# MLA stage of a two-layer block: transposes of two probability blocks together in every even unit

## The reference

```python
def attend(blk):
    qn, qr = blk
    s = (jnp.einsum('bqhd,bkhd->bhqk', qn, k_nope, preferred_element_type=jnp.float32)
         + jnp.einsum('bqhr,bkr->bhqk', qr, k_rope, preferred_element_type=jnp.float32)) * scale
    p = jax.nn.softmax(s, axis=-1).astype(v.dtype)
    return jnp.einsum('bhqk,bkhd->bqhd', p, v)
o = lax.map(attend, (to_blocks(q_nope), to_blocks(q_rope)))
```

## Time and profile before

| | us |
|---|---|
| median of 3 runs | 3247.91 (3247.35 to 3248.86) |
| the profiled execution | 3250.53 |
| its span, first to last instruction | 3248.9 |
| TensorE busy | 3220.4 |
| VectorE, ScalarE, GpSimd busy | 1803.5, 1305.8, 630.8 |

### The profile page before, as it was taken

One profiled execution on the slowest core, in us unless ns is written; L12 is line 12 of the kernel. 1 busy time (PEld: TensorE's weight loads), 2 busy tenths in 40 slices (PEclk: granted clock), 3 DMA queues, 4 the chain that ended last, 5 costly groups with the idle time before them and its releaser, 6 DMA issues.

```text
span 3248.9 us, 38219 instructions
## 1 busy us (share of the span) xinstructions
PE 3220.4 (99%) x15436; PEld 2691.3 (83%) x15436; DVE 1803.5 (56%) x2728; ACT 1305.8 (40%) x1991; POOL 630.8 (19%) x502
## 2 busy tenths in 40 slices
PE   9999999999999999999999999999999999999998
PEld 7888888888888888888888888888888888788887
DVE  6865775444448655845443465554544268974433
ACT  5653553332237534633322323332332248743221
POOL 1521231111005311520110022111111014521101
PEclk9999999999999999999999999999999999999999
DMA  4122323323221122322233222222223223223222
GB/s 137 38 81 65 109 93 104 100 99 100 96 93 59 60 75 90 109 94 95 96 99 107 91 81 81 82 91 91 97 92 100 95 81 102 91 89 101 97 98 85
DMA packets 85136, 295.60 MB, mean 91 GB/s; under 512 B 9568, under 2 KB 12128, under 8 KB 84960
## 3 DMA queue, kind: packets, MB, share of 16 engines
q1 hardware_dynamic: 84384, 292.76, 27.4%
q10 hardware_dynamic: 576, 0.40, 0.0%
HBM read 291.02 MB, written 2.10 MB: 90 GB/s over the span
## 4 chain that ended last, share of the span: by engine, by line
PE 85%; DVE 8%; ACT 3%; issue 1%; POOL 1%; DMA 1%; SPq 0%; ACTq 0%; DVEq 0%; POOLq 0%
PE bank L313 84%; DVE wl L569 2%; PE bank L316 2%; DMA raw<-in_wts 1%; DVE small L1299 1%; ACT m_p L536 1%; POOL u_g L591 1%; ACT wh L533 1%; DVE u_uc L565 0%; DVE m_ptl L569 0%; DVE c_kl L569 0%; DVE m_qf L559 0%; DVE m_sh L809 0%; DVE u_h L3283 0%; ACT m_pth L533 0%
## 5 line engine op out<-in xcount | busy, mean ns | idle before, releaser
L569 DVE TENSOR_TENSOR wl<-raw,wh 128x1024 fp32r<-128x1024 f32 (+1 forms) x531 | 660.1, 1246 | 761.7 <-ACT wh L533 760.8
L313 PE MATMUL bank<-zh,wh 128*128 128x512 f32 (+1 forms) x2652 | 1025.9, 387 | 6.2 <-ACT zh L533 6.2
L313 PE MATMUL bank<-zh,wl 128*128 128x512 f32 (+1 forms) x2652 | 1020.7, 385 | 1.9 <-DVE wl L569 1.9
L313 PE MATMUL bank<-zl,wh 128*128 128x512 f32 (+1 forms) x2652 | 1019.1, 384 | 1.7 <-DVE zl L572 1.6
L533 ACT ACTIVATE wh<-raw 128x1024 fp32r<-128x1024 f32 (+1 forms) x531 | 555.9, 1052 | 531.4 <-PE bank L313 469.0
L313 PEld LDWEIGHTS bank<-zh,wl 128*128 128x128 f32 x2652 | 499.6, 188 | 107.2 <-DVE wl L569 7.2
L313 PEld LDWEIGHTS bank<-zh,wh 128*128 128x128 f32 x2652 | 500.0, 189 | 102.5 <-ACT zh L533 6.2
L313 PEld LDWEIGHTS bank<-zl,wh 128*128 128x128 f32 x2652 | 500.0, 189 | 98.2 <-DVE zl L572 3.0
L313 PE MATMUL bank<-f_mh,wh 128*128 128x512 f32 (+1 forms) x748 | 285.1, 381 | 0.0
L313 PE MATMUL bank<-f_mh,wl 128*128 128x512 f32 (+1 forms) x748 | 283.3, 379 | 0.0
L313 PE MATMUL bank<-f_ml,wh 128*128 128x512 f32 (+1 forms) x748 | 280.7, 375 | 0.0
(11 more groups left out here) (337 smaller groups left out, 4474.3 us busy)
## 6 DMA issues: line engine op xcount, KB each, us to landing
raw<-in_wts SPq DMA_DIRECT2D x529, 512.0 KB, 3.3
c_nb<-in_c_bias SPq DMA_DIRECT2D x16, 384.0 KB, 3.2
x<-in_xT SPq DMA_DIRECT2D x8, 256.0 KB, 6.2
out<-x SPq DMA_DIRECT2D x13, 128.0 KB, 1.8
b_mask<-in_b_mask SPq DMA_DIRECT2D x2, 576.0 KB, 4.5
r_d<-in_decay SPq DMA_DIRECT2D x4, 256.0 KB, 2.9
raw<-in_wts SPq DMA_DIRECT2D x2, 256.0 KB, 3.7
m_t<-in_mla_tab SPq DMA_DIRECT2D x2, 256.0 KB, 4.7
```

The source lines that it names most:

```text
L313: return self.e.matmul(out, l, r, start=start, stop=stop, skip_group_check=inside)
L569: return self.e.tensor_tensor(out, src, b32(hi), ALU.subtract)
```

## The change

- TensorE: from unit 4 on, each even unit i transposes blocks i - 4 and i - 3, one group of four after the other, ahead of its scores; odd units transpose nothing. Unit 33 goes, and block 30 is transposed in unit 34 beside 31.
- The tuple of tiles from `fill` is (0, 2, 0, 1, 1, 2, 0, 2), where it was (0, 1, 1, 1, 2, 1, 1, 1): odd units take more, even ones fewer; eight in eight units, as before.
- ScalarE copies block i - 4 in iteration i, not block i - 3.
- VectorE makes the low half of block i - 4 in iteration i: in odd iterations ahead of the reduction, in even ones behind it, where the low half was always.

```diff
--- before.py
+++ after.py
@@ -1207,8 +1207,7 @@
     rest, q = fill(), queries()
 
     def unit(i):
-        if 3 <= i < 35:
-            j = i - 3
+        for j in (i - 4, i - 3) if 4 <= i < 35 and i % 2 == 0 else ():
             ps = L.claim(turn_bank(j), "lo", "pt", "mla", l, j)
             L.wait_ge("sc", "mla", l, j)
             for kt in range(4):
@@ -1241,12 +1240,12 @@
             next(q, None)
         if i % 8 == 3 and i < 24:
             tensor_k(L, l, i // 8 + 1)
-        for _ in range((0, 1, 1, 1, 2, 1, 1, 1)[i % 8]):
+        for _ in range((0, 2, 0, 1, 1, 2, 0, 2)[i % 8]):
             next(rest, None)
 
     for i in range(32):
         unit(i)
-    return {0: lambda: unit(32), 1: lambda: unit(33), 2: lambda: unit(34), 4: lambda: unit(36)}
+    return {0: lambda: unit(32), 2: lambda: unit(34), 4: lambda: unit(36)}
 
 
 def turn_bank(j):
@@ -1261,8 +1260,8 @@
             scalar_b(L, ("b", l, 0) + MLA_FILL[i // 8 - 1])
         if i >= 9 and i % 4 == 1:
             scalar_y_move(L, m.m_yt, (i - 9) // 4, "mla", l)
-        if 3 <= i < 35:
-            j = i - 3
+        if 4 <= i < 36:
+            j = i - 4
             hb = j // 2
             L.wait_ge("tp", "mla", l, j)
             if hb > 1:
@@ -1286,6 +1285,16 @@
     L.ahead()
 
 
+def vector_pt_lo(L, l, i):
+
+    m, j = L.m, i - 4
+    if 0 <= j < 32:
+        hb = j // 2
+        hi, lo = [f4(x)[:, :, 128 * (j % 2):128 * (j % 2) + 128] for x in m.m_pt[hb % 2]]
+        L.wait_ge("hi", "pt", "mla", l, j)
+        L.lo(lo, f4(m.bank[turn_bank(j)]), hi).then_inc(*L.tell("lo", "pt", "mla", l, j))
+
+
 def vector_mla(L, l):
     m = L.m
     L.lead = 0
@@ -1293,6 +1302,8 @@
         level = L.level
         if i == 29:
             vector_y_add(L, m.m_yt, m.m_yf, 5, "mla", l)
+        if i % 2:
+            vector_pt_lo(L, l, i)
         if i < 32:
             c = i % 8
             L.wait_ge("qk", "mla", l, i)
@@ -1301,12 +1312,8 @@
             vector_mv(L, l, (0, 3, 1, 2)[i])
         if i >= 9 and i % 4 == 1 and i != 29:
             vector_y_add(L, m.m_yt, m.m_yf, (i - 9) // 4, "mla", l)
-        if 3 <= i < 35:
-            j = i - 3
-            hb = j // 2
-            hi, lo = [f4(x)[:, :, 128 * (j % 2):128 * (j % 2) + 128] for x in m.m_pt[hb % 2]]
-            L.wait_ge("hi", "pt", "mla", l, j)
-            L.lo(lo, f4(m.bank[turn_bank(j)]), hi).then_inc(*L.tell("lo", "pt", "mla", l, j))
+        if i % 2 == 0:
+            vector_pt_lo(L, l, i)
         if i < 32:
             vector_div(L, i, "mla", l)
         L.ahead_of(level)
```

## The result

The changed kernel takes 3278.42 us (median of 4 runs, 3277.48 to 3279.72), the kernel before beside it 3247.75 us. The ratio is 1.0095, 95% interval 1.0083 to 1.0106: 30.7 us more. The forecast was 3271.4, a loss of 23.5 us: direction and range held, and 7.2 us of the loss were missing.

A forecast was written before the change was run, and what follows sets the result against it. TensorE, 99% busy, bounds the kernel, but in MLA VectorE's lengthened loop would set the pace: 11.8 us per layer, 23.6 for two, less 0.1 for switches, on 3247.9 gives 3271.4 us; range 3257 to 3281 (80%).

The forecast's parts named there:

- The bound: MLA: VectorE's serial loop through ScalarE would set the pace, walked unit by unit at 26.4 us per eight units against 22.4.
- Eight transposes together: TensorE in MLA: grouping removes 32 switches between transposes and products; saving taken as 0, upper bound 2.6 us.
- the sum for switches: Closing total: 0.1 us subtracted for switches from 23.6 us, giving +23.5 us.
- Weight tiles dealt anew: TensorE's tiles in MLA: new dealing evens out units, costs nothing itself; still eight tiles per eight units.
- Low half ahead of the reduction: VectorE, odd MLA iterations: low half leaves the exp's cover and waits for its copy; 4.0 us more per eight units.
- keeps its place before the exp: ScalarE in MLA: remark that the copy m_pth, now a unit on, stays ahead of the exp; no cost given.
- The order of SP's loads is the same, so TensorE's own work does not change: SP's load queue: unchanged order was taken to leave TensorE's work as it was, at no cost.
- the banded stage that follows, which I take as unchanged: Stage after MLA: assumed to take the same time; a time change there was named as a sign of error.
- The clock: Rival for both MLA stages: TensorE's clock falls to its lower level for half of them, 3355 us; chance 2%.
- The signs in the profile: MLA: five expected traces, among them m_ptl waits nearly every even unit, 10 to 13 us per layer, and TensorE busy 85.
- Faster: Rival in MLA: vanished m_pth waits pay for uncovered low halves, stalls go, switches save up to 2.6; 3240 us, chance 6%.
- No change: Rival in MLA: VectorE's loop lengthens by less than its lead, TensorE stays the bound; 3247.9 within 6 us, chance 8%.

The follow-up runs named there:

- experiment 7: Changed kernel, but both copies and both low halves of a pair made in the even iteration, behind the reduction, none in odd ones: 3254.89 us, ratio to before 1.0020.
- experiments 4 and 9: Changed kernel with the old dealing of tiles: 3277.77 us; kernel before with the new dealing alone: 3247.82 us.
- experiment 2: Kernel before, with VectorE's low half (block i - 3) ahead of the reduction in odd iterations: 3271.06 us, ratio to before 1.0072.
- experiment 6: Kernel before, with copies and low halves of block i - 4 instead of i - 3 in iteration i, behind the reduction: 3272.50 us, ratio to before 1.0075.
- experiment 3: Changed kernel, with SP's b_mask load waiting for the transposes of block 30, not the low half of block 31: 3272.89 us.
- experiment 1: Changed kernel, with the low half of odd blocks behind the reduction again, as for even blocks: 3268.25 us, ratio to before 1.0063.

## Why the prediction was right, and where it was short

- *The bound.* Right: VectorE, 56% busy on the page, sets the pace of MLA through its round trip to ScalarE. Its walk gave 26.4 us for eight units, and 26.5 was traced; reductions 16, 24 and 31 were walked at 112.9, 139.3 and 160.6 and came at 113.22, 139.73 and 161.13; the late start after the stage was 11.9 for 11.4.
- *Eight transposes together.* Right: nothing saved (experiment 7). The walk took 0 for a switch and yet took 0.1 off the sum for switches; that term has no source, and it changes nothing. The Trainium skill ("TensorE: Matmul & The Clock Gate", Part 2) has only an isolated product pay for its drain, while in a stream it is hidden. The rows of experiment 7 agree: 0.67 and 1.11 us leave no break at a change between transposes and products.
- *Weight tiles dealt anew.* Right: nothing, in either kernel (experiments 4 and 9).
- *Low half ahead of the reduction.* The mechanism holds (experiment 2, 23 us by itself). But "Here the price sits" said too much: undoing it returned only 10 us. The part on the dealing passed over the copies' move with "keeps its place before the exp", and that move, which takes a unit of lead from the low half, costs 24 us alone (experiment 6, where it falls on every block; in the changed kernel it falls on odd ones). The two causes don't add: the late mask load apart, which is about 5 us of the changed kernel, either of them makes up most of the loss, and with the low halves early and half of them covered 6.5 us are left (experiment 7). The total came out because the walk followed the whole order; its attribution to one edit was wrong.
- *"The order of SP's loads is the same, so TensorE's own work does not change", and "the banded stage that follows, which I take as unchanged".* Here the number fell short. The order was the same, but the time at which SP passes a load was not: b_mask waits for the low half of block 31. It is 1.65 and 1.73 us of wait in the two layers, and 5.5 us in the whole between medians (experiment 3). Of the missing 7.2 another 1.3 lie in the stages, which came 0.4 and 0.9 us longer than walked; the last 0.4 is within the spread of the runs.
- *The clock.* The rival had the fall as 2% and as half of both stages. It did fall, for 3.4 us at a time, three times a layer, and that is a small term and not a case of its own: inside the stages it is at most part of the 1.3 us above. "I expect no fall" was wrong. The row of 1.15 us idle was a poor bound, since waits of the changed kernel reach 2.1 us.
- *The range.* Its upper end is worked out as 3280 and given as 3281; 3278.4 lies close below either, and the central figure is the better witness for the walk.
- *The signs in the profile.* Waits for m_ptl were nine rather than "nearly every even unit", with 9.4 us where 10 to 13 were named; the reciprocals of odd units idle 0.85 us as said; "TensorE's busy time in it still 85" was wrong (89.5), mostly by the clock.
- *The rivals.* "Faster" fell: the waits for m_pth did not vanish, they rose from 6.4 to 10.5 us. "No change" fell as its counter-argument had it: VectorE was 4.3 us late by reduction 16 already (113.22 for 108.97), and nothing gave that back.

## What to carry to other kernels

Where an engine's chain runs through another one and back, ask of each instruction whether it lies under the round trip, and how many iterations ahead of its reader it is made: moving it out of the cover or taking one iteration of lead each cost 23 to 24 us here, though every engine had idle time. Before pairing instructions to save switches, read what a switch costs from two starts; here it was nothing. When an event is moved, look for every wait on it, also in queues of other stages, since all that stands behind it moves as well.

## What the runs showed of the hardware

TensorE's granted clock fell to its lower level (0.50) for 3.4 us at a time in the first layer of the changed kernel, after waits of 1.97 us (twice, inside MLA) and 1.65 us (banded stage). In the kernel before, a wait of 1.15 us left it at 1.00. But the length of the wait alone does not decide. In the second layer of the same execution a wait of 1.97 us left the clock at 1.00:

```profile
1076.28 0.66 PE L316 MATMUL bank<-ident,m_p 128*128 128x128 f32 x4 [1.97 <-DVE m_ptl L569]
...
1076.28:1080.00 3.72, 3.72 (x22) 1.00 0.32 124
```

So did the wait of 1.65 us ahead of b_k<-b_q in the first layer of experiment 1. What decides between them stays open.

Transposes of 128 x 128 go at 0.11 us each among themselves and beside products alike (experiment 7 and the earlier trace rows).
